# Two more weight units split, VectorE's tap sums in PSUM, and a part of the taps on GpSimd, in a decoder trunk of one core

## What is computed

```python
# layer 0
a, bv, bg, z = split(rms_norm(x) @ w_in0)          # 1024, 1024, 1024, 2048 columns
ya = per_group_matmul(trailing_mean(a) - a) * pool_scale
u  = causal_depthwise_conv(bv * sigmoid(bg), width 31) + conv_b
yb = silu(layer_norm(u))
x  = x + (concat(ya, yb) * silu(z)) @ w_out0
# layer 1
q, k, v, z = split(rms_norm(x) @ w_in1)            # 16 heads of 64, q and k normalised
x  = x + (attention(q, k, v, alibi, causal) * silu(z)) @ w_out1
```

## Time and profile before

| | us |
|---|---|
| median of 3 runs (332.34 to 332.8) | 332.65 |
| the profiled execution, its own time | 333.14 |
| its span, first to last instruction | 331.3 |
| TensorE busy | 325.0 (98%) |
| VectorE busy | 256.2 (77%) |
| ScalarE busy | 230.4 (70%) |
| GpSimd busy | 51.8 (16%) |

### The profile page before, as it was taken

How to read it: one execution, slowest core, us unless ns; L and a number is a source line. 1 busy time by engine, 2 the same in 40 slices (tenths; PEclk the granted TensorE clock), 3 DMA queues, 4 the chain that set the end, 5 groups by cost and what they waited for, 6 DMA issues and landing times.

```text
span 331.3 us, 5760 instructions
## 1 busy us (share of the span) xinstructions
PE 325.0 (98%) x2212; PEld 296.2 (89%) x2212; DVE 256.2 (77%) x475; ACT 230.4 (70%) x429; POOL 51.8 (16%) x58
## 2 busy tenths in 40 slices
PE   8999999999999999999999999999999999999995
PEld 8899999999989999997999999988887776778885
DVE  2699989999689999996886898747556877748633
ACT  4677999994999897935775557824756666575630
POOL 0050024424422310120000000005500231400000
PEclk9999999999999999999999999999999999999999
DMA  7979488979999998676629343780634323200003
GB/s 277 409 272 357 146 267 217 202 164 349 276 252 345 167 380 296 130 174 208 254 103 403 130 133 133 279 347 10 245 127 166 135 99 132 108 0 2 2 0 127
DMA packets 12842, 64.77 MB, mean 195 GB/s; under 512 B 1424, under 2 KB 1552, under 8 KB 6544
## 3 DMA queue, kind: packets, MB, share of 16 engines
q1 hardware_dynamic: 8064, 53.78, 43.2%
q0 software_dynamic: 4608, 10.49, 17.3%
q10 hardware_dynamic: 144, 0.15, 0.2%
HBM read 52.88 MB, written 1.05 MB: 163 GB/s over the span
## 4 chain that ended last, share of the span: by engine, by line
PE 93%; DMA 3%; ACT 1%; DVE 1%; issue 1%; POOL 0%; ACTq 0%; POOLq 0%
PE bank L1058 25%; PE bank L1060 23%; PE bank L1059 23%; PE bank L1118 5%; PE bank L1092 4%; DMA w_lo<-raw 3%; PE bank L1166 2%; PE bank L1272 2%; PE bank L1299 2%; PE bank L1135 2%; PE bank L1126 2%; PE bank L1285 2%; PE bank L1251 1%; ACT scratch L467 1%; DVE scratch L752 1%
## 5 line engine op out<-in xcount | busy, mean ns | idle before, releaser
L723 DVE TENSOR_TENSOR w_lo<-raw,w_hi 128x1024 fp32r<-128x1024 f32 x76 | 90.3, 1222 | 19.6 <-ACT w_hi L459 19.4
L1058 PE MATMUL bank<-h_hi,w_hi 128*128 128x256 f32 x304 | 86.6, 285 | 0.4 <-DMA w_lo<-raw 0.4
L459 ACT CAST w_hi<-raw 128x1024 fp32r<-128x1024 f32 x84 | 84.4, 1048 | 2.7 <-PE bank L1060 2.7
L1060 PE MATMUL bank<-h_hi,w_lo 128*128 128x256 f32 x304 | 86.0, 283 | 0.0
L1059 PE MATMUL bank<-h_lo,w_hi 128*128 128x256 f32 x304 | 86.0, 283 | 0.0
L1058 PEld LDWEIGHTS bank<-h_hi,w_hi 128*128 128x128 f32 x304 | 58.3, 192 | 0.9 <-issue 0.8
L1059 PEld LDWEIGHTS bank<-h_lo,w_hi 128*128 128x128 f32 x304 | 58.3, 192 | 0.1
L1060 PEld LDWEIGHTS bank<-h_hi,w_lo 128*128 128x128 f32 x304 | 58.3, 192 | 0.0
L841 DVE SCALAR_TENSOR_TENSOR scratch<-scratch,params 128x256 f32<-128x256 f32 x108 | 44.1, 484 | 0.2
L1058 PE MATMUL bank<-w_hi,h_hi 128*128 128x512 f32 x96 | 39.2, 408 | 0.0
L1058 PE MATMUL bank<-ya_hi,w_hi 128*128 128x256 f32 x128 | 38.1, 297 | 0.0
(11 more groups left out here) (106 smaller groups left out, 549.0 us busy)
## 6 DMA issues: line engine op xcount, KB each, us to landing
raw<-w SPq DMA_DIRECT2D x49, 1024.0 KB, 6.3
side_v<-side_ring POOLq DMA_DIRECT2D x24, 256.0 KB, 8.2
w_lo<-raw POOLq DMA_DIRECT2D x8, 512.0 KB, 8.1
X<-xT SPq DMA_DIRECT2D x2, 512.0 KB, 5.2
out<-X SPq DMA_DIRECT2D x4, 256.0 KB, 2.6
consts<-const SPq DMA_DIRECT2D x1, 290.0 KB, 13.5
params<-vec ACTq DMA_DIRECT2D x1, 149.0 KB, 4.9
```

Source lines behind the costliest of these rows:

```text
L459: nc.scalar.copy(halves(w_hi, cut_slot(n), half), halves(raw, n % RAW, half)).then_inc(hi_cut, 1)
L723: nc.vector.tensor_tensor(halves(w_lo, cut_slot(n), half), halves(raw, n % RAW, half), halves(w_hi, cut_slot(n), half).bitcast(F32), ALU.s ...
L1058: nc.tensor.matmul(dst, wh, ah, start=start, stop=False, skip_group_check=True)
L1060: return nc.tensor.matmul(dst, wl, ah, start=False, stop=stop, skip_group_check=True)
```

## The change

- Units 9 and 13 leave `NATIVE` and are split; units up to 17 rotate over four places of `w_hi` and `w_lo` instead of three.
- The sums that VectorE adds taps to live in banks 4 to 7 of PSUM up to unit 15 (`partial`); ScalarE's first taps go there too.
- GpSimd builds a second sum of each pair in V: it makes a first tap (`tensor_scalar`, two tiles) and adds twelve products, which ScalarE makes into three places of PR (`pool_home`). `pool_gate` makes GpSimd wait, in each slot, for VectorE's last subtraction or last window.
- In slot 15 VectorE merges both sums of each pair into V (L921), after which all goes on in V. TensorE's unit 16 waits for the fourth merge, since it writes the same banks.
- GpSimd's side DMAs move a slot later, and unit 14's casts move in front of the copy of A[3] on ScalarE.
- ScalarE's remaining products move to other buffers (YP, PR, and from slot 14 those freed by the windows).

```diff
-NATIVE = frozenset((0, 9, 13, 16, 21, 23, 25))
+NATIVE = frozenset((0, 16, 21, 23, 25))
...
+FOUR, SLOT_ORDER = ZA[1], (3, 2, 0, 1)
...
+    if n > FOUR:
+        return (cut_index(n) - (n > SPARE) - cut_index(Z1[0]) + 1) % 3
+    return SLOT_ORDER[(cut_index(FOUR) - cut_index(n)) % 4]
...
+MERGE_SLOT = PW - 1
+POOL_ADDS = {4: (0, 0, 0), 6: (0, 1), 9: (1, 2), 10: (2,), 11: (3,), 13: (3,), 14: (2, 3)}
+POOL_STARTS = {3: (0,), 5: (1,), 7: (2,), 9: (3,)}
...
+def pool_gate(n):
+
+    if n - 1 in A:
+        return "pooled", n - A[0]
+    return ("cut", 2 * low_cuts(n + 2) + 2) if n + 2 not in NATIVE and n + 2 not in ADDED else None
...
+        def partial(tiles):
+
+            c = tiles[0]
+            at = S * (c % 2)
+            t = bank[4 + c // 2][:, at:at + S * len(tiles)]
+            return t.rearrange("p (c t) -> p c t", c=2) if len(tiles) == 2 else t
...
+            def pool_conv(n):
+
+                gate = pool_gate(n)
+                if gate and (POOL_PLAN[n - 1] or n in POOL_START):
+                    pool.wait_ge(pooled if gate[0] == "pooled" else lo_cut, gate[1])
+                for pair, k, made, ready, _ in POOL_PLAN[n - 1]:
+                    pool.wait_ge(pool_tap, ready)
+                    pool.wait_ge(pool_product, made)
+                    nc.gpsimd.tensor_tensor(V[:, 2 * pair:2 * pair + 2, :], V[:, 2 * pair:2 * pair + 2, :],
+                                            pool_home(made), ALU.add).then_inc(pool_tap, 1)
+                for pair, k in POOL_START.get(n, ()):
+                    pool.wait_ge(u_ready, pair + 1)
+                    for c in CONV_PAIRS[pair]:
+                        nc.gpsimd.tensor_scalar(V[:, c, :], U[:, c, k:k + S], column(CW + TAPS * c + k), None,
+                                                ALU.mult).then_inc(pool_tap, 1)
+
+            for n in range(BG[1], OA[0]):
+                if BG[1] < n <= MERGE_SLOT:
+                    side_sums(n - 1)
+                    if n + 2 in EARLY_ADDED:
+                        added_low(n + 2)
+                if BG[1] < n <= MERGE_SLOT:
+                    pool_conv(n)
+                if n >= MERGE_SLOT:
+                    side_sums(n)
...
-                        nc.scalar.activation(V[:, c, :], U[:, c, 0:S], ACT.Identity, bias=column(CB + c),
+                        nc.scalar.activation(partial((c,)), U[:, c, 0:S], ACT.Identity, bias=column(CB + c),
...
+                    total = partial(tiles) if done <= MERGED else V[:, c:c + 2, :] if len(tiles) == 2 else V[:, c, :]
+                    if k is None and product is None:
+                        dve.wait_ge(pool_tap, POOL_LAST[c // 2])
+                        nc.vector.tensor_tensor(V[:, c:c + 2, :], total, V[:, c:c + 2, :], ALU.add).then_inc(tap, 1)
...
                 if g == 0:
                     pe.wait_ge(root_ready, 1)
+                    pe.wait_ge(tap, MERGED)
```

More of the change, by code:

```diff
@@ L113, in slot_free @@
     if n == SPARE:
-        return released(PW)
+        return released(max(m for m in CUTS if m <= FOUR and cut_slot(m) == CUT - 1))
     if n == Z1[3]:
@@ L192, in conv_plan @@
 def conv_plan():
-    plan, last, used, count, before, late, folded = {}, {}, [], 0, None, None, []
-    left = {pair: [k for k in range(1, TAPS) if k not in side_taps(pair)] for pair in range(4)}
+    plan, last, used, count, before, late, folded, homes, free_at = {}, {}, [], 0, None, None, [], [], []
+    left = {pair: list(range(1, FIRST_POOL[pair] - POOL_TAKEN[pair] + 1)) for pair in range(4)}
     folds = [2 * pair + (SIDE_ITEMS + i) % 2 for pair in range(SIDE) for i in range(2)]
@@ L203, in conv_plan @@
         act_time = min(act_time, ACT_CARRY) + ACT_SHARE * length - act
+        for pair in range(4) if n == MERGE_SLOT else ():
+            tiles = CONV_PAIRS[pair]
+            count += 1
+            plan[n].append((tiles, None, None, max(last[c] for c in tiles), count))
+            dve_time -= 0.61
+            last.update({c: count for c in tiles})
+        if n == MERGE_SLOT:
+            merged = count
         while dve_time > 0 or n == OA[0]:
@@ L216, in conv_plan @@
                 used.append(count)
+                ring = next(homes for first, homes in reversed(RINGS) if n >= first)
+                homes.append(ring[len(homes) % len(ring)])
+                free_at.append(max([u for u, h in zip(used[:-1], homes[:-1]) if h == homes[-1]], default=0))
                 dve_time, act_time = dve_time - 0.61, act_time - 0.8
@@ L425, in added_low, with side_sums @@
                                    accum_op=ALU.add).then_inc(lo_added[i][half], 16)
-            for n in range(BG[1], OA[0]):
+            def side_sums(n):
                 for pair, item in side_items(n):
@@ L536, in _ @@
                         continue
-                    if product == LATE_FROM:
+                    if HOMES[product] > 4:
                         act.wait_ge(pooled, 4)
-                    if product_free(product):
-                        act.wait_ge(tap, product_free(product))
+                    if FREE_AT[product]:
+                        act.wait_ge(tap, FREE_AT[product])
                     for i, c in enumerate(tiles):
@@ L550, in _ @@
                             act.wait_ge(u_ready, n // 2)
-                        nc.scalar.activation(V[:, c, :], U[:, c, 0:S], ACT.Identity, bias=column(CB + c),
+                        nc.scalar.activation(partial((c,)), U[:, c, 0:S], ACT.Identity, bias=column(CB + c),
                                              scale=column(CW + TAPS * c)).then_inc(first_tap, 1)
+                for pair, k, made, _, _ in POOL_PLAN.get(n, ()):
+                    if made > 3:
+                        act.wait_ge(pool_tap, POOL_USED[made - 4])
+                    for i, c in enumerate(CONV_PAIRS[pair]):
+                        last = nc.scalar.mul(pool_home(made)[:, i, :], U[:, c, k:k + S], column(CW + TAPS * c + k))
+                    last.then_inc(pool_product, 1)
                 if n in BG:
@@ L827, in taps @@
             def taps(n):
-                for tiles, k, product, ready, _ in CONV_PLAN.get(n, ()):
+                for tiles, k, product, ready, done in CONV_PLAN.get(n, ()):
                     c = tiles[0]
```

64 lines of the change are left out of this document (37 added, 27 removed).

## The result

| | before | after |
|---|---|---|
| median of 5 runs each on the same chip | 332.65 us | 337.12 us (336.85 to 338.57) |
| ratio, 95% interval | | 1.0142 (1.0123 to 1.0162) |
| profiled execution | 333.14 us around a span of 331.3 | 337.01 us around a span of 335.2 |
| mean granted clock of TensorE | 1.0 | 0.995 |
| units 9, 13 | 6.9 us each | 5.8 us each |

The forecast was slower by 1.5 us, 334.1, with a range up to 336.5. The direction came out, the size did not, and the range missed the result.

What follows compares the result with a forecast made beforehand. The prediction took TensorE, busy 98%, as the bound and unit 16's start as deciding: the later of two chains, 108.0 against 106.5 before, gave +1.5 us, so 332.65 + 1.5 = 334.1 us, range 330.3 to 336.5.

Steps and rivals of the forecast that it cites:

- The splits' gain, 2.3 us, and TensorE's arrival: Splitting units 9 and 13 saves TensorE 2 x 1.15 = 2.3 us; it arrives at unit 14 at 91.9.
- Up to the first window: ScalarE's first pool copy comes at 65.6 instead of 63.73; VectorE finishes the first pool window at 71.0.
- The second round of the ring, 77.3: Ring of four pool units: ScalarE copy and cast, VectorE subtraction and window, next copy; second window done at 77.3.
- the prediction's own sign of being wrong: Listed signs of error included VectorE subtractions of over 1.3 us while GpSimd adds (the port).
- GpSimd blocks VectorE: Rival: GpSimd's second add delays unit 12's subtraction, 0.9 us more in both chains, 335.0 us; chance 0.11.
- The third round: Unit 13's casts and subtractions are new in the ring: third window at 84.5 instead of 80.9, copy 3 at 85.6.
- GpSimd's queue: An add (1.2) and two side DMAs (1.8) precede unit 14's load: issue 87.5, landing 8.1 later, stall 3.7 us.
- Behind that unit (5.8 ...): unit 16 starts 12.4 after unit 14.: After unit 14 come Silu, unit 17's cast, subtractions and merges; unit 16 starts 12.4 us after unit 14, at 108.0.
- The other chain, 107.1: VectorE's last window, taps into PSUM, subtractions, product adds and merges end at 107.1, where unit 16 would start.
- PSUM: PSUM operands cost VectorE nothing (taps 0.396 us); rival: dearer taps, 2.5 us more, 335.8 us, chance 0.10.
- Everything after unit 16 shifts by one amount: Work behind unit 16 stays TensorE-bound, so its start decides the time; the mean's fold keeps its cover.
- The late DMA: Rival: unit 14's load takes 10 to 11.7 us to land, giving 336.0 to 337.8 us; chance 0.12.

Runs made afterwards that it cites:

- f_nat13: The changed kernel with unit 13 native again and nothing else: 338.20 us.
- c_warm: The changed kernel with 18 extra matmuls of ones on TensorE in front of unit 14: 336.23 us.
- a_low14: The changed kernel with unit 14's low-half loads issued one slot sooner in GpSimd's queue, ahead of its add for the third window: 337.04 us.
- x4: The changed kernel with unit 13 native, unit 14's loads and casts sooner, merges ahead of unit 17's subtractions, GpSimd's last first taps in slot 8: 332.73 us.
- e_split: The kernel before with only units 9 and 13 split, no taps in PSUM and nothing new on GpSimd: 343.63 us.
- p_noadds: The changed kernel without GpSimd's adds of products (VectorE makes these taps), GpSimd's first taps kept: 344.44 us.

## Why the forecast was right in direction and wrong in size

- **The splits' gain, 2.3 us, and TensorE's arrival.** Right: units 9 and 13 at 5.8, unit 14 awaited at 91.5 (92.1 with the offset; forecast 91.9).
- **Up to the first window.** Right: copy at 65.10 plus 0.5 (65.6), window done at 70.6 plus 0.5 (71.1; forecast 71.0).
- **The second round of the ring, 77.3.** Wrong by 1.7 us, the first step that failed: the sum had nothing for GpSimd holding VectorE up. 0.9 is the subtraction held up by GpSimd's adds, 0.35 the window held up by its first taps, 0.4 the product that waited for those. A subtraction of 2.08 us beside a GpSimd add is also the prediction's own sign of being wrong. The first was my rival "GpSimd blocks VectorE", to the tenth (0.9), with a chance of 0.11 where it should have been the forecast: the row showed GpSimd finishing with VectorE's subtraction, which is coupling, and I read it as going one way. The Trainium skill (SBUF — State Buffer, section SBUF: two separate sides) says that whoever started first holds the pair of ports. The trace agrees for the add, which started at 71.95, ahead of the subtraction at 72.26. It agrees less well for the first tap: its record starts at 73.23, but a subtraction that starts at 74.26 took its usual 1.21 us, and the tap ended only at 76.18. ScalarE's wait of 3.0 us was in no sum of mine: I had followed the gates of GpSimd's adds but not which of its operations reaches the count that a product waits for.
- **The third round, 7.0 us long.** Right to the tenth (78.63 to 85.65), and unit 13's casts are its new part, as f_nat13 shows (2.4 us).
- **GpSimd's queue.** The add took 1.29 us (1.2), the two side DMAs under 1.2 (1.8), the landing 7.9 us (8.1). Issue at 88.10 plus 0.5 against 87.5, the gap 4.6 against 3.7.
- **"Behind that unit (5.8 ...): unit 16 starts 12.4 after unit 14."** This is the second step that failed, by 1.6 us: it took 14.0. Unit 14 lasted 7.2 instead of 5.7 because the clock was down after the gap; the 6.5 us behind the unit came out as forecast. My forecast had a gap of 3.7 us and gave it no price but its length. c_warm measures the clock's part at 1.5 us in unit 14 and 1.3 at unit 16.
- **The other chain, 107.1.** It exists (a_low14, f_nat13, x4), and I had it as the lower of two. Without its wait of 1.82 us VectorE would have ended the merges at 108.2, 108.7 with the offset, which is 107.1 and the ring's 1.7. What I missed is that a chain so close behind takes back most of what a single move gains.
- **PSUM.** Taken at nothing, measured at nothing: that rival is out.
- **Everything after unit 16 shifts by one amount.** Right, 221.0 against 220.9 us from there to the last matmul; e_split and p_noadds show that the cover there is real, and that GpSimd's adds supply it.
- **The range.** With the port's 1.7 less the 0.6 saved in the queue, and the 1.5 of the clock, the same sum gives 332.65 + 1.5 + 1.1 + 1.5 = 336.8 us. The late DMA did not happen. With the ring's slip alone the sum is 335.2, inside the range; what carried the time out of it is the clock, for which neither the sum nor a rival had a term. The direction was not luck: the wait for the DMA at unit 14, from which it was forecast, is there and is the largest term.

Left open: which of the adds' operands the port contention hangs on was not tried, nor was the cast order alone or the count of `pool_tap` put right. Open too is why a gap of 1.9 us lowered the clock in a_low14 while one of 2.4 us, in the same run at unit 16, did not.

## What to carry to other kernels

When a helper's chain ends in a wait of TensorE, price the wait, then the clock behind it, then look for the chain that is second by a microsecond or two: one move alone gave 0.1 to 0.9 us here by the medians, three and a cast order together 4.6. When engines share work by a planner's averages, look at what it puts in front of a fixed point (here the four merges) and move load behind it, if there is slack there; six taps were worth 1.5 us. For every wait count on a shared engine ask which of its operations reaches that count, in the order in which it makes them, not only when it may start.
